# Suffix sums as products of rounded parts, a tile's output products moved into the last decode turn, and state copies in pieces: one decoder step on one core

## The reference, cut to what matters

```python
def stick_breaking_weights(z, mask):
    log_keep = jnp.where(mask, jax.nn.log_sigmoid(-z), 0.0)
    later = lax.cumsum(log_keep, axis=z.ndim - 1, reverse=True) - log_keep
    return jnp.where(mask, jnp.exp(jax.nn.log_sigmoid(z) + later), 0.0)
...
    qa, ka, va, qd, kd, vd = split_projections(x_prompt, w_in)
    o_sb_p = sb_prompt(qa, ka, va, sb_logit_bias)          # 8 heads, 512 positions, head size 64
    o_dil_p = merge_by_denominator(outs_p, lses_p)         # 8 more heads, dilated windows
    y_prompt = finish_layer(x_prompt, o_sb_p, o_dil_p, w_out, ...)
...
    o_sb_s = sb_sample(qa_s, ka_s, va_s, k_past, v_past, sb_logit_bias)   # 8 sequences, 2048 cached positions
    kc = jnp.concatenate([state_k_win, kd_s], axis=1)      # window buffers, copied on by 4 rows
    vc = jnp.concatenate([state_v_win, vd_s], axis=1)
...
    h1 = layer_norm(DN_ALPHA * x + mixed, ln1_g, ln1_b)    # mixed = concat(o_sb, o_dil) @ w_out
```

## Time and profile before

| | us |
|---|---|
| median of 3 runs (lowest, highest) | 2474.9 (2467.79, 2475.26) |
| profiled execution, its own time | 2474.16 |
| its span, first to last instruction | 2472.3 |
| PE busy in the span | 2304.7 (93%) |
| DVE busy | 1549.5 (63%) |
| ACT busy | 942.2 (38%) |
| POOL busy | 393.3 (16%) |

### The profile page before, as it was taken

The page is one execution under the profiler, slowest core; times in us unless marked ns, Lnnn a source line. Parts: engine busy times, 40 slices in busy tenths (PEclk is TensorE's granted clock), DMA queues, the critical chain, the costliest instruction groups (busy, mean ns, idle before and its releaser), DMA issues.

```text
span 2472.3 us, 37860 instructions
## 1 busy us (share of the span) xinstructions
PE 2304.7 (93%) x12921; PEld 1901.2 (77%) x12921; DVE 1549.5 (63%) x3167; ACT 942.2 (38%) x1432; POOL 393.3 (16%) x370
## 2 busy tenths in 40 slices
PE   7998988998999798999899889999999999999996
PEld 7997765666566446985577688999989899999895
DVE  4352331333444434678998778777777777777777
ACT  3225542444444512223355633333333333333332
POOL 0001000000000000000000044333333333333320
PEclk9999987889999898999999999999999999999998
DMA  4226977877766621203254699999999999999982
GB/s 130 87 88 224 332 237 271 275 263 263 267 207 209 196 66 37 83 21 106 92 197 178 243 333 342 317 313 315 314 313 311 316 315 311 312 313 313 311 294 78
DMA packets 224111, 568.20 MB, mean 230 GB/s; under 512 B 18065, under 2 KB 96466, under 8 KB 221330
## 3 DMA queue, kind: packets, MB, share of 16 engines
q1 hardware_dynamic: 174994, 327.75, 40.2%
q0 software_dynamic: 49024, 239.23, 27.6%
HBM read 528.24 MB, written 105.12 MB: 256 GB/s over the span
## 4 chain that ended last, share of the span: by engine, by line
PE 79%; DVE 8%; DMA 4%; ACT 3%; SPq 3%; issue 2%; POOL 0%; ACTq 0%; DVEq 0%
PE psum L2065 20%; PE psum L2056 16%; PE psum L405 7%; PE psum L1560 5%; PE psum L1839 5%; PE psum L2046 3%; DMA sample<-in_cache_v_sb_dram 3%; PE psum L1862 3%; PE psum L1420 3%; PE psum L1001 3%; PE psum L1055 2%; PE psum L991 2%; PE psum L1073 2%; PE psum L1023 1%; SPq L926 1%
## 5 line engine op out<-in xcount | busy, mean ns | idle before, releaser
L2065 PE MATMUL psum<-expert_parts 128*128 128x512 f32 x2304 | 550.3, 394 | 0.8 <-DVE expert_parts L2184 0.8
L2065 PEld LDWEIGHTS psum<-expert_parts 128*128 128x128 f32 x2304 | 426.7, 188 | 87.3 <-DVE expert_parts L2184 1.8
L2056 PE MATMUL psum<-h_parts,expert_parts 128*128 128x384 f32 x2304 | 444.5, 341 | 2.9 <-DVE expert_parts L2179 1.5
L2056 PEld LDWEIGHTS psum<-h_parts,expert_parts 128*128 128x128 f32 x2304 | 403.0, 189 | 10.9 <-issue 1.8
L2126 ACT ACTIVATE expert_parts<-peer 128x1024 fp32r<-128x1024 f32 x128 | 135.8, 1061 | 358.9 <-PE psum L2065 332.8
L2179 DVE TENSOR_TENSOR expert_parts<-psum,expert_parts 128x512 fp32r<-128x512 f32 x192 | 132.8, 692 | 147.2 <-ACT expert_parts L2120 147.2
L2222 DVE SCALAR_TENSOR_TENSOR kept<-experts,kept 128x1024 f32<-128x1024 f32 x160 | 205.0, 1281 | 8.3 <-DMA experts<-in_peer_v_dram,kept 3.0
L2031 POOL DMA_INDIRECT experts<-in_peer_v_dram,kept x160 | 192.6, 1204 | 70.5 <-issue 47.5
L1839 PE MATMUL psum<-h_whole,gate_table 128*128 128x384 f32 x512 | 180.6, 497 | 10.5 <-ACT gate_table L1891 10.5
L1331 DVE TENSOR_TENSOR sample_parts<-sample,sample_parts 128x512 fp32r<-128x512 f32 x128 | 85.5, 690 | 166.9 <-ACT sample_parts L1184 166.5
L405 PE MATMUL psum<-projection_parts 128*128 128x256 f32 (+1 forms) x1440 | 174.5, 283 | 3.8 <-DVE projection_parts L511 3.8
(11 more groups left out here) (281 smaller groups left out, 3287.1 us busy)
## 6 DMA issues: line engine op xcount, KB each, us to landing
peer<-in_peer_v_dram SPq DMA_DIRECT2D x128, 512.0 KB, 5.0
peer<-in_peer_u_dram SPq DMA_DIRECT2D x96, 512.0 KB, 5.4
sample<-in_cache_k_sb_dram SPq DMA_DIRECT2D x128, 256.0 KB, 3.9
sample<-in_cache_v_sb_dram SPq DMA_DIRECT2D x128, 256.0 KB, 3.0
out_dram<-in_state_k_win_dram POOLq DMA_DIRECT2D x8, 4088.0 KB, 54.4
out_dram<-in_state_v_win_dram POOLq DMA_DIRECT2D x8, 4088.0 KB, 41.2
gates_dram<-gate_table SPq DMA_DIRECT2D x12, 2048.0 KB, 7.3
experts<-gates_dram SPq DMA_DIRECT2D x32, 768.0 KB, 6.8
```

The costliest lines, as they stand in the source:

```text
L2056: last = pe.matmul(bank(6)[:, 0:ND], lhsT=u_t[s][:, a, k, :], rhs=h1_r[:, b, k, 0:ND], start=(k == 0 and n == 0), stop=(k == KD - 1 and n ...
L2065: last = pe.matmul(bank(2 * t + half), lhsT=weight[s][:, a, t * P:(t + 1) * P], rhs=v_r[s][:, b, half * 512:(half + 1) * 512], start=(firs ...
```

## The change

There are three parts. First, the suffix sums of the prompt: DVE rounds `softplus(h)` to fp32r and subtracts the rounded part to get the rest (two more operations over 1280 columns in each head, and the triangle and the ones are rounded once), and PE multiplies both parts, twenty fp32r products in place of ten fp32 ones. `sb_z` gets a fourth buffer. PE makes `scores(h+2)` behind the sums of `h` instead of `scores(h+1)` ahead of them. Second, the `w_out` products of token tile 0 move into the decode's last turn, eight ahead of that turn's sums and eight behind them. Third, the five late window copies are cut into four pieces each, and a piece waits for pages 0, 4, 8 or 12 of its turn to be scored.

```diff
-        sb_z = [take(WIDE) for _ in range(3)]
+        sb_z = [take(WIDE) for _ in range(4)]
...
             scores(0)
+            scores(1)
             for h in range(H):
-                if h + 1 < H:
-                    scores(h + 1)
                 pe.wait_ge(sem("sb_softplus"), h + 1)
                 if h >= 1:
                     pe.wait_ge(sem("sb_exponents"), h)
-                sp_h = sb_p[h % 2]
                 for kb in range(KB):
                     r = region(kb)
-                    last = pe.matmul(bank(3, 3)[:, r], lhsT=tri, rhs=sp_h[:, r], start=True, stop=(kb == KB - 1))
+                    for x in range(2):
+                        last = pe.matmul(bank(3, 3)[:, r], lhsT=tri_r, rhs=sp_r[h % 2][:, x, r], start=(x == 0),
+                                         stop=(kb == KB - 1 and x == 1))
...
                 last.then_inc(sem("sb_sums"), 1)
+                if h + 2 < H:
+                    scores(h + 2)
                 if h >= 1:
                     weigh(h - 1)
...
-                dve.scalar_tensor_tensor(sb_p[h % 2], sb_z[h % 3], 0.0, sb_e[h % 2], ALU.max, ALU.add)\
+                st.link(dve.scalar_tensor_tensor(sb_p[h % 2], sb_z[h % 4], 0.0, sb_e[h % 2], ALU.max, ALU.add))
+                st.link(dve.tensor_copy(sp_r[h % 2][:, 0, :], sb_p[h % 2]))
+                dve.tensor_tensor(sp_r[h % 2][:, 1, :], sb_p[h % 2], sp_r[h % 2][:, 0, :], ALU.subtract)\
                     .then_inc(sem("sb_softplus"), 1)
...
             logits(0)
             softplus(0)
+            logits(1)
             for h in range(H):
-                if h + 1 < H:
-                    logits(h + 1)
                 dve.wait_ge(sem("sb_sums"), h + 1)
...
                 if h + 1 < H:
                     softplus(h + 1)
+                if h + 2 < H:
+                    logits(h + 2)
...
+            def mix_first(half):
+                if half == 0:
+                    pe.wait_ge(sem("w_out_in"), KD * 16)
+                    pe.wait_ge(sem("page_copied"), PAGES * DB + 2)
+                for k in range(KD):
+                    last = pe.matmul(bank(half), lhsT=o_t[:, k, 0:P], rhs=wo_sb[:, k, half * 512:(half + 1) * 512],
+                                     start=(k == 0), stop=(k == KD - 1))
+                if half == 1:
+                    last.then_inc(sem("mixed"), 1)
...
                         if s == SUMS_AT:
+                            if not pages:
+                                mix_first(0)
                             sums(b - 1)
+                            if not pages:
+                                mix_first(1)
...
-                if b >= 1 and 3 + b < len(MOVES):
-                    move_state(pool, 3 + b)
+                if 1 <= b <= 2 * DB - MOVED:
+                    for piece in range(PIECES):
+                        pool.wait_ge(sem("page_scored"), PAGES * b + 4 * piece + 3)
+                        move_state(pool, MOVED + b - 1, piece, PIECES)
...
-            for t in range(NT):
+            for t in range(1, NT):
```

More of the change, by code:

```diff
@@ L559, in build @@
         o_nat = take(4 * D).rearrange("p (t d) -> p t d", t=4)
+        sp_r = [sums_tensor[:, 2 * e * WIDE:2 * (e + 1) * WIDE].rearrange("p (x n) -> p x n", x=2) for e in range(2)]
+        tri_r, ones_r = (sums_tensor[:, 4 * WIDE + e * P:4 * WIDE + (e + 1) * P] for e in range(2))
         counts = take(4 * SEQ).rearrange("p (t k) -> p t k", t=4)
@@ L562, in build, with move_state @@
         bias_ht = small[:, 8:40].rearrange("p (h t) -> p h t", h=H)
-        MOVES = (11, 0, 0, 0, 1, 1, 1, 1, 1)
-        def move_state(pool, turn):
-            for n in range(sum(MOVES[:turn]), sum(MOVES[:turn + 1])):
-                b = n // 2
-                to, frm = ((k_win_sample, state_k_win), (v_win_sample, state_v_win))[n % 2]
-                pool.dma_start(to[b].rearrange("w h d -> (w h d)")[0:(WIN - DT) * DH],
-                               frm[b].rearrange("w h d -> (w h d)")[DT * DH:WIN * DH]).then_inc(sem("window_moved"), 16)
+        MOVED, PIECES = 11, 4
+        def move_state(pool, n, piece=0, pieces=1):
+            b = n // 2
+            to, frm = ((k_win_sample, state_k_win), (v_win_sample, state_v_win))[n % 2]
+            size = (WIN - DT) * DH // pieces
+            at = piece * size
+            pool.dma_start(to[b].rearrange("w h d -> (w h d)")[at:at + size],
+                           frm[b].rearrange("w h d -> (w h d)")[DT * DH + at:DT * DH + at + size])\
+                .then_inc(sem("window_moved"), 16)
         def region(kb):
@@ L584, in _ @@
             pool.wait_ge(sem("counts_in"), 2 * 16)
-            move_state(pool, 0)
+            for n in range(MOVED):
+                move_state(pool, n)
             pool.wait_ge(sem("v_sb_out"), 2 * 16)
@@ L608, in weigh @@
                         a = AT[kb] + (qb - kb) * P
-                        last = pe.matmul(out[:, qb * HD:(qb + 1) * HD], lhsT=sb_z[h % 3][:, a:a + P],
+                        last = pe.matmul(out[:, qb * HD:(qb + 1) * HD], lhsT=sb_z[h % 4][:, a:a + P],
                                          rhs=v_n["sb"][:, kb, h * HD:(h + 1) * HD], start=(kb == 0), stop=(kb == qb))
@@ L620, in _ @@
                     pe.wait_ge(sem("sb_exponents"), h)
-                sp_h = sb_p[h % 2]
                 for kb in range(KB):
                     r = region(kb)
-                    last = pe.matmul(bank(3, 3)[:, r], lhsT=tri, rhs=sp_h[:, r], start=True, stop=(kb == KB - 1))
+                    for x in range(2):
+                        last = pe.matmul(bank(3, 3)[:, r], lhsT=tri_r, rhs=sp_r[h % 2][:, x, r], start=(x == 0),
+                                         stop=(kb == KB - 1 and x == 1))
                     for later in range(kb + 1, KB):
                         a = r.start + (later - kb) * P
-                        last = pe.matmul(bank(3, 3)[:, a:r.stop], lhsT=ones, rhs=sp_h[:, region(later)],
-                                         start=False, stop=(later == KB - 1))
+                        for x in range(2):
+                            last = pe.matmul(bank(3, 3)[:, a:r.stop], lhsT=ones_r, rhs=sp_r[h % 2][:, x, region(later)],
+                                             start=False, stop=(later == KB - 1 and x == 1))
                 last.then_inc(sem("sb_sums"), 1)
+                if h + 2 < H:
+                    scores(h + 2)
                 if h >= 1:
@@ L642, in log_part @@
                     act.wait_ge(sem("sb_softplus"), h - 1)
-                st.link(act.activation(e, sb_z[h % 3], ACT.Abs))
+                st.link(act.activation(e, sb_z[h % 4], ACT.Abs))
                 st.link(act.activation(e, e, ACT.Exp, scale=-1.0))
@@ L657, in _ @@
                 act.wait_ge(sem("sb_exponents"), h + 1)
-                act.activation(sb_z[h % 3], sb_z[h % 3], ACT.Exp).then_inc(sem("sb_weights"), 1)
+                act.activation(sb_z[h % 4], sb_z[h % 4], ACT.Exp).then_inc(sem("sb_weights"), 1)
                 if h >= 1:
```

18 lines of the change are left out of this document (11 added, 7 removed).

## The result

The changed kernel takes 2487.7 us, the median of 13 runs (2474.2 to 2495.8); the kernel before takes 2472.6 in 13 runs beside it (2458.1 to 2487.6). The ratio is 1.0049, 95% interval 1.0029 to 1.0068: some 12 us slower (7 to 17; the two medians lie 15.1 apart), where 2472 and no change that can be measured had been forecast. The execution that was profiled took 2490.02 us, its span is 2488.2.

The account below looks back on a forecast made before the run. PE was taken to bound the prompt at 9.62 us a head, DVE and ACT's loop 1.36 behind and binding after the change. 2474.2 + 12.5 - 14.9 + 0 = 2471.8, said as 2472; range 2461 to 2486.

Parts of the forecast that it names:

- the price of part three: Decode: five turns with pieces at 2 us each, +10 against 10.0 saved; 0 in all, between -10 and +12.
- a little for piece three, all 3 for piece four: Decode steps 9 to 15: delay by late value pages, for the upper end of 0 to 4.4 us a turn.
- its slower rival: Decode: pieces meet value pages in all five turns, 4.4 x 5 - 10 = +12, so 2484 us; chance 0.21.
- what goes: Decode: the whole late copies in four turns cost 10.0 us at most, which can be got back.
- 10.64: Prompt attention: us per head set by the DVE and ACT loop, with cast, subtraction and waits added to 8.26.
- 285.51 + 12.3: Prompt attention: start of head 7's sums before, plus 12.3 us of lateness forecast by then.
- +12.5: Prompt attention in all, in us, half clock included; bounds +5 and +17.
- 1 to 3 us: Prompt attention's tail: what half clock would add there.
- the 10.8 that stood there without the clock: Prompt attention: lateness of the next stage in us, before half clock was added.
- -14.9: Part two: w_out stage loses 13.87 us, last turn 1.0 (bounds -1.7 and +1.5); total between -12.4 and -15.6.
- 1.5 had been worked out: Last decode turn: value products start 1.5 us later than before, behind mix_first(1), at no cost to ACT's page 4 split.
- the forecast's -2.4: Whole kernel: the three parts together, +12.5 - 14.9 + 0 us, giving 2471.8.

Follow-up runs that it names:

- pieces_only: The kernel before with only the five late copies cut in four pieces each, waiting for pages 0, 4, 8, 12: ratio 1.0065, +16 us.
- the two experiments on the loop: Kernel before with rounded sums: cast and subtraction moved outside DVE's loop, ratio 0.9983; or subtraction and the rest's ten products left out, 0.9972.
- sums_only: The kernel before with only the rounded suffix sums and scores two heads ahead: ratio 1.0065, about +16 us.
- copies_in_w_out: The kernel before with tile 0's products in the last turn and the late copies issued one per token tile in the w_out stage: ratio 0.9952.
- mix_only: The kernel before with only tile 0's w_out products moved into the last decode turn: ratio 0.9941, -14.6 us.
- pieces_early: The kernel before with the late copies in pieces that wait for pages 0, 2, 4 and 6: ratio 0.9982, -4.5 us.
- sums_loop: The kernel before with rounded sums reordered on DVE, ACT and PE, cast and subtraction outside DVE's loop with ACT: ratio 0.9983.

## Why the prediction was wrong

**The step that failed is the price of part three.** The forecast put a turn with pieces at 0 to 4.4 us ("a little for piece three, all 3 for piece four" makes the upper end), took 2 from between without a row for it, and named 4 us per turn as the point from which its slower rival decides. Measured against no late copies, a turn with pieces costs (313.6 - 291.6)/5 = 4.4 us in the changed kernel and 5.3 in `pieces_only`; 3.8 and 3.2 of this are PE's idle time, the rest is time at half clock, which differs between executions. For what goes, 10.0 had been worked out, and before stands 300.7 - 291.6 = 9.1 above no copies, of which 5.2 are idle time. So part three is +13 in the changed kernel and +17.5 in `pieces_only` (by idle time alone +13.7 and +10.9), instead of 0: at and beyond the upper bound of +12. The mechanism was the one described; its size was taken too small for two reasons that the traces show. Piece three hurts about as much as piece four: over the five turns PE idles 9.0 us more than without late copies between the scoring of pages 8 and 12, and 9.8 more behind page 12 (7.1 and 9.0 in `pieces_only`). And I had ended the path at ACT's wait and PE's value products; DVE's key copy stands behind the page's split, which stops PE's transposes too, and 12.3 of the 18.7 us by which PE's two waits grew are on that copy.

The Trainium skill, "DMA: Bandwidth & Descriptors", section "Queues, rings and completion order", has an engine drain a whole packet of one queue before it serves the next, and by that part three was to lie near its upper bound. The runs agree: it lay at +13. They show the lateness behind a piece, not the order inside an engine, so why a load is late behind a piece stays open.

**The prompt was right in mechanism and near in size**: 10.57 us per head against 10.64, sums of head 7 at 298.2 against 285.51 + 12.3 = 297.8. The head did not change with PE's clock, and the two experiments on the loop confirm it. The stage came out at +14.6 instead of +12.5, within +5 to +17. Of the 2.1 us between, 1.7 lie in the tail, 13.7 us at half clock from start to end, where 1 to 3 us had been allowed on 10.3; in `sums_only`, at 0.84, the tail takes 9.5 us and the stage is 10 us late, near the 10.8 that stood there without the clock. The twenty rounded products took 2.83 us at full clock against 2.8. Two slips in the working change nothing here: the bounds of this part come out at +5.9 and +17.8 by its own prices, not +5 and +17, and its 0.05 us for 128 columns is the 0.06 of the quotient beside it.

**Part two was right in its mechanism and, by these two traces, 2.7 us too high.** The stage is 12.1 shorter and the last turn 0.1: -12.2 against -14.9. Two terms are off. The first tile that stays in the stage takes 15.68 us, because it begins at half clock, where before the first tile ran at full speed; that is 1.8, and it is a matter of the execution rather than of the change. Without part two the `w_out` stage takes 80.6 us in the two executions where it began at full clock and 81.9 to 82.3 in the five where it began at 0.57 to 0.60; with part two it takes 66.6 in the one at full clock and 68.4 to 68.8 in the five at 0.50 to 0.57 (`copies_in_w_out`, with its late drain, is left aside). Like against like, that is some 14.0 and 13.4 less, the 13.9 that was forecast, and with it goes the ratio of `mix_only` (-10.6 to -18.8 us). The other term is the last turn, which gained 0.1 (0.3 in `mix_only`) in place of 1.0. The first value product comes 15.5 us behind the turned outputs, 14.5 before: 1.0 later, where 1.5 had been worked out. ACT then waits 3.15 us for it ahead of its split of page 4, but that split starts 16.6 us behind the outputs, 17.2 before, so that the lateness cost nothing up to there, as forecast; the 0.7 gained is lost again behind it, and where is not shown.

**The sum by what was measured**: 14.6 - 12.2 + 14.4 + 1.2 (turn 7) = +18 at the start of the stage behind `w_out`, and +15.9 in the span, because the rest took 2.4 less in this execution; the runs say +12 (7 to 17). Of the distance of that +18 to the forecast's -2.4, part three makes 12.9, the two other parts 4.8; turns 6 and 7, which have no piece, make 2.7. The forecast for "slower" is what happened, by its own mechanism; it had 0.21. What spoke against it was that a whole copy had cost only 2.5 us a turn. But those were issued ahead of the value pages, as the early pieces of `pieces_early` were, and so say little of pieces that come among them. The nearest row for pieces three and four was the lateness of page loads under a copy, divided by four, on pages without slack; it gave the 3 us of lateness that came behind each. Of these, PE lost some 2 for each piece.

## What to carry to other kernels

Before a background transfer is cut up and spread, ask of each piece which loads it will meet and how many buffers those have: here a piece that met loads with slack cost next to nothing, one that met loads without slack 1.6 to 1.9 us of PE's idle time, and the same bytes ranged from nothing to 8 us a turn by the page they waited for. When a busy engine's work is made shorter, measure the loop that comes second first; two DVE operations inside it turned a PE gain into a loss, and with the same operations outside it, and the lists of ACT and PE put in order for that, there was none. Behind that loop stood a third bound, the copies that the stage's end waits for. A wait that names a neighbouring engine should be followed back through that engine's queue to what was really late.

## What the runs showed of the hardware that was not expected

- POOL's drain at a stage's end lasts until its own DRAM-to-DRAM copy has landed: 14.7 us from the issue of the last copy to the next stage in `copies_in_w_out`, with copies that take 14.4 to 18.0 to land. At the end of the prompt attention POOL's drain ends 1.3 to 1.5 us behind the landing of the last early copy in all fourteen traces. A transfer that nobody reads can so hold up every engine at a stage's end, as it did for some 4 us in `sums_loop`.
- A piece of 1022 KB lands in 5.4 to 8.6 us (median 7.0), where a whole copy of 4088 KB took 18.4: a quarter of the bytes takes more than a quarter of the time.
- A cast of 128x1280 to fp32r on DVE takes 0.83 us, the same as a plain copy of that size.
